# The second output projection's third and fourth chunk as a pair of seven products, with the weights in the five shared load slots

## What is computed

```python
    o = o.reshape(B, S, SB_WIDTH) * jax.nn.silu(zg)
    return o @ w_out            # 256 x 2048 by 2048 x 2048, fp32
...
        h = h + y
    return rms_norm(h, final_g)
...
        xn = rmsnorm(x, norm_mix_pre[l])
        proj = jnp.einsum('bsd,dc->bsc', xn, w_in[l])
```

## Time and profile before

| | us |
|---|---|
| three runs | 2550.94 median (2549.61 to 2550.96) |
| the profiled execution | 2550.57 |
| its span, first to last instruction | 2548.6 |
| PE busy in it | 2542.5 |
| DVE busy in it | 1865.1 |
| ACT busy in it | 1323.7 |

### The profile page before, as it was taken

How to read it: one execution, slowest core, us unless ns; L and a number is a source line. 1 busy time by engine, 2 the same in 40 slices (tenths; PEclk the granted TensorE clock), 3 DMA queues, 4 the chain that set the end, 5 groups by cost and what they waited for, 6 DMA issues and landing times.

```text
span 2548.6 us, 29599 instructions
## 1 busy us (share of the span) xinstructions
PE 2542.5 (100%) x11383; PEld 2107.5 (83%) x11383; DVE 1865.1 (73%) x2181; ACT 1323.7 (52%) x1585; POOL 34.9 (1%) x56
## 2 busy tenths in 40 slices
PE   9999999999999999999999999999999999999999
PEld 7888888888888888888888888888888888888887
DVE  6866567566866666776866876778678789899796
ACT  6654444444555555455444544445565456465563
POOL 1000000000000000000000000000020000000000
PEclk9999999999999999999999999999999999999999
DMA  8766776676787777778566787666757676667674
GB/s 282 210 204 197 210 208 193 196 207 198 209 225 201 216 195 205 219 217 231 165 183 181 206 225 198 205 206 198 241 171 230 191 212 209 218 201 230 195 229 157
DMA packets 534796, 527.43 MB, mean 207 GB/s; under 512 B 294896, under 2 KB 297824, under 8 KB 534656
## 3 DMA queue, kind: packets, MB, share of 16 engines
q1 hardware_dynamic: 531856, 518.09, 68.4%
q0 software_dynamic: 2384, 6.93, 1.1%
q10 hardware_dynamic: 416, 0.52, 0.1%
HBM read 488.24 MB, written 2.10 MB: 192 GB/s over the span
## 4 chain that ended last, share of the span: by engine, by line
PE 97%; DVE 2%; SPq 0%; DMA 0%; ACT 0%; issue 0%; DVEq 0%
PE bank L2429 29%; PE bank L2431 29%; PE bank L2430 29%; PE bank L2496 2%; PE bank L2498 2%; PE bank L2497 2%; DVE t_wl L1310 1%; PE bank L2615 1%; PE bank L2604 1%; PE bank L2594 1%; SPq L548 0%; DMA t_stage<-in_a_w_in_dram 0%; PE bank L2537 0%; PE bank L2550 0%; PE bank L2543 0%; DVE t_ytl L1359 0%
## 5 line engine op out<-in xcount | busy, mean ns | idle before, releaser
L1310 DVE TENSOR_TENSOR t_wl<-t_stage,t_wh 128x1024 fp32r<-128x1024 f32 x837 | 1012.1, 1221 | 479.8 <-ACT t_wh L726 472.8
L726 ACT ACTIVATE t_wh<-t_stage 128x1024 fp32r<-128x1024 f32 x838 | 878.0, 1057 | 753.5 <-PE bank L2431 696.9
L2429 PE MATMUL bank<-t_wl,t_xth 128*128 128x512 f32 x2320 | 909.9, 392 | 0.4 <-DVE t_xtl L1352 0.4
L2431 PE MATMUL bank<-t_wh,t_xtl 128*128 128x512 f32 x2320 | 903.0, 389 | 0.0
L2430 PE MATMUL bank<-t_wh,t_xth 128*128 128x512 f32 x2320 | 902.8, 389 | 0.0
L2431 PEld LDWEIGHTS bank<-t_wh,t_xtl 128*128 128x128 f32 x2320 | 435.5, 188 | 90.9
L2429 PEld LDWEIGHTS bank<-t_wl,t_xth 128*128 128x128 f32 x2320 | 435.6, 188 | 90.4 <-DVE t_xtl L1352 0.9
L2430 PEld LDWEIGHTS bank<-t_wh,t_xth 128*128 128x128 f32 x2320 | 435.7, 188 | 89.6 <-issue 0.2
L2429 PE MATMUL bank<-t_wl,t_yth 128*128 128x512 f32 x882 | 343.4, 389 | 0.1
L2430 PE MATMUL bank<-t_wh,t_yth 128*128 128x512 f32 x882 | 342.7, 389 | 0.0
L2431 PE MATMUL bank<-t_wh,t_ytl 128*128 128x512 f32 x882 | 342.7, 389 | 0.0
(11 more groups left out here) (441 smaller groups left out, 1810.3 us busy)
## 6 DMA issues: line engine op xcount, KB each, us to landing
t_stage<-in_a_w_in_dram SPq DMA_DIRECT2D x182, 512.0 KB, 4.4
t_stage<-in_w_in_dram SPq DMA_DIRECT2D x168, 512.0 KB, 4.2
t_stage<-in_b_w_in_dram SPq DMA_DIRECT2D x128, 512.0 KB, 4.4
t_stage<-in_w_down_dram SPq DMA_DIRECT2D x92, 512.0 KB, 5.3
t_stage<-in_w_up_dram SPq DMA_DIRECT2D x91, 512.0 KB, 4.5
t_stage<-in_a_w_out_dram SPq DMA_DIRECT2D x60, 512.0 KB, 4.4
t_ubuf<-in_w_up_dram SPq DMA_DIRECT2D x37, 512.0 KB, 4.6
t_ubuf<-in_w_down_dram SPq DMA_DIRECT2D x36, 512.0 KB, 5.3
```

What stands on the lines that cost most here:

```text
L726: e.activation(wh[:, j % N_SPLIT], stage[s], ACT.Copy).then_inc(*hi(j))
L1310: e.tensor_tensor(low, src, high.bitcast(F32), ALU.subtract).then_inc(*lo(j))
L2429: e.matmul(o, h, w_l, start=start, stop=False)
L2431: return e.matmul(o, l, w_h, start=False, stop=stop)
```

## The change

The pair is added to `halved_pairs`, `sums_of` and `quarters` name the places of its sums and its partial results (parts of `vreg` and the buffers 0 and 1), and no slots are opened for it. The work of ACT and DVE around `b_out` is put in another order, with the pieces of the `a_out` pair; the row products of chunks 2 and 3, their squares and the scales go behind the gained parts.

```diff
@@ halved_pairs
             [(("a_out", h, 2), ("a_out", h, 3)) for h in range(2)] +
+            [(("b_out", 2), ("b_out", 3))] +
@@ sums_of
+        if name[0] == "b_out":
+            return ("zg",), mtl[:, 0:4, :], mtl[:, 4:8, :], vreg[:, 5120:6144]
@@ quarters
-        if kind in ("gm", "up", "a_out"):
+        if kind in ("gm", "up", "a_out", "b_out"):
@@ scalar
-        for c in range(4):
+        def hb_squares(c):
             slot(end("b_out", c) + 2)
             e.wait_ge(*vec.at("hb", c))
             for i in range(2):
                 squares(hres[:, i, cols(c)], ssq[:, i, c:c + 1], "hb", c, i)
+
+        def final_squares(c):
             for i in range(2):
                 e.wait_ge(*vec.at("final", c, i))
                 squares(hres[:, i, cols(c)], ssq2[:, i, c:c + 1], "final", c, i)
-            slot(end("b_out", c) + (5 if c == 3 else 4))
+
+        slot(end("b_out", 0) - 2)
+        sum_high("zg")
+        hb_squares(0)
+        final_squares(0)
+        slot(end("b_out", 0) + 4)
+        gained_highs(0, gmix, "x2", 0)
+        hb_squares(1)
+        apart(first_of["b_out", 2], turned.at("zg", 3))
+        slot(end("b_out", 1) + 4)
+        gained_highs(1, gmix, "x2", 1)
+        slot(end("b_out", 1) + 7)
+        final_squares(1)
+        hb_squares(2)
+        hb_squares(3)
+        for c in (2, 3):
+            slot(end("b_out", 3) + (2, 5)[c - 2])
             gained_highs(c, gmix, "x2", c)
+        final_squares(2)
+        final_squares(3)
@@ vector
+        def to_result(m):
+
+            e.wait_ge(*vec.at("w", "pair", m))
+            for n in range(2):
+                d = hres[:, :, cols(pairs[m][n][1])]
+                e.tensor_tensor(d, d, buf[n], ALU.add).then_inc(*vec("early", m, n))
+                e.wait_ge(*vec.at("early", m, n))
+
+        slot(end("b_out", 0) - 3)
+        split_sums(yth, ytl, vreg[:, 4096:5120], vreg[:, 5120:6144], "zg")
+        slot(end("b_out", 0) - 1)
+        sum_low("zg")
+        out_sum(0)
+        out_turn(0)
+        final_row(0)
+        out_sum(1)
+        out_turn(1)
+        gained_lows(0, gmix, "x2", 0)
+        m = first_of["b_out", 2]
+        slot(end("b_out", 1) + 3)
+        together(m, turned.at("zg", 3))
+        final_row(1)
+        slot(end("b_out", 1) + 6)
+        gained_lows(1, gmix, "x2", 1)
+        slot(end("b_out", 1) + 7)
+        to_result(m)
+        out_sum(2)
+        out_turn(2)
+        out_sum(3)
+        e.wait_ge(*vec.at("hb", 3))
+        e.memset(pad[:, :, 0:3], 0.0).then_inc(*vec("pad0"))
+        out_turn(3)
+        slot(end("b_out", 3) + 2)
+        gained_lows(2, gmix, "x2", 2)
+        slot(end("b_out", 3) + 5)
+        gained_lows(3, gmix, "x2", 3)
+        final_row(2)
+        final_row(3)
...
```

More of the change, by code:

```diff
@@ L182, in _program @@
     mtl, _ = sb("mtl", [128, 16, S], F32R, offset=v_at + 16384)
-    vtile = (vreg[:, 1024:2048].rearrange("p (a b) -> p a b", a=2), vreg[:, 5120:6144].rearrange("p (a b) -> p a b", a=2))
+    vtile = [vreg[:, n:n + 1024].rearrange("p (a b) -> p a b", a=2) for n in (1024, 5120)]
     stage = [stage_[:, i] for i in range(N_STAGE)] + [ubuf[:, 0], ubuf[:, 1], spare[:, 0], spare[:, 1], pool4[:, 3], rowb,
@@ L1739, in vector, with out_sum @@
         zg_low(3)
-        for c in range(4):
+        def out_sum(c):
             slot(end("b_out", c))
@@ L1746, in vector, with out_turn @@
                 e.tensor_tensor(hr, hr, accs("b_out", c)[i], ALU.add).then_inc(*vec("hb", c) if i else vec())
-            if c == 3:
-                e.wait_ge(*vec.at("hb", 3))
-                e.memset(pad[:, :, 0:3], 0.0).then_inc(*vec("pad0"))
+        def out_turn(c):
             slot(end("b_out", c) + 1)
@@ L1752, in vector, with final_row @@
             turn_chunk(lambda i: hres[:, i, cols(c)], flat[zt_buf[c]], "x2", c)
+        def final_row(c):
             slot(end("b_out", c) + 2)
@@ L1759, in vector @@
                 e.tensor_tensor(hr, hr, rowb[:, c % 2, :], ALU.mult).then_inc(*vec("final", c, i))
[L1760 to L1776, removed]
@@ L1777, in vector @@
-            slot(end("b_out", c) + (5 if c == 3 else 4))
-            gained_lows(c, gmix, "x2", c)
+        def to_result(m):
[6 more added lines that the diff above has]
+        split_sums(yth, ytl, vreg[:, 4096:5120], vreg[:, 5120:6144], "zg")
@@ new lines, in vector @@
+        out_sum(3)
[8 more added lines that the diff above has]
+        final_row(3)
+        both = rq[:, 1, 0:4]
+        v12, v1 = both[:, 0:2], both[:, 2:4]
+        eps1 = rq[:, 0, 4:6]
+        e.tensor_reduce(v1, ssq[:, :, 0:4], AX, ALU.add).then_inc(*vec())
@@ new lines, in vector @@
+        after_own()
+        e.tensor_scalar(v1, v1, 1.0 / D, EPS, ALU.mult, ALU.add).then_inc(*vec())
+        after_own()
+        e.tensor_scalar(eps1, v1, EPS, None, ALU.mult).then_inc(*vec())
+        e.wait_ge(*square.at("final", 3, 1))
+        e.tensor_reduce(v12, ssq2[:, :, 0:4], AX, ALU.add).then_inc(*vec())
+        after_own()
+        e.scalar_tensor_tensor(out=v12, in0=v12, scalar=1.0 / D, in1=eps1, op0=ALU.mult,
+                               op1=ALU.add).then_inc(*vec())
+        rsqrt(s12_1, both, 4)
@@ L1781, in vector @@
+        after_own()
+        e.tensor_scalar(h12, s12, 0.5, None, ALU.mult).then_inc(*vec("h12"))
         slot(when(428))
```

## The result

The kernel with the pair takes **2556.32 us** (median of 14 runs, 2554.50 to 2557.66), the kernel before 2550.48 (14 runs, 2549.59 to 2551.73). The ratio is 1.0022, 95% interval 1.0015 to 1.0029: about 5.8 us slower, where +3.04 on the profiled execution was forecast. The profiled execution took 2556.42 us, with a span of 2554.7.

The account below looks back on a forecast made before the run. TensorE, busy the whole span, was taken as the bound: matmuls by their pace. -1.36 + 1.64 + 1.74 + 1.02 = +3.04 us gave 2553.6 for the profiled execution, 2554.0 as median; range 2550.3 to 2557.5.

Parts of the forecast that it names:

- The gain: PE, first four K tiles of chunks 2 and 3: 42 matmuls instead of 48, -1.36 us.
- The first wait: PE at chunk 1's last group waits for its weights' low part, whose load waits for a slot: +1.64 us.
- low part P6 after a 0.4 wait: DVE's queue after the second weight difference: product P6's low part was to come after waiting only 0.4.
- The walk: Four queues followed in program order with trace durations, from DVE's low part at 1099.39; it gave the three waits.
- The second wait: PE's `begin` at chunk 3's first group waits for chunk 1's addition, queued on DVE behind low parts: +1.74 us.
- The third wait: PE at chunk 2's group at K tile 8 waits for a low part behind DVE's queued work: +1.02 us.
- The load time: The critical loads of the first two waits: 3.8 us taken from a quiet stretch, 3.6 and 5.0 as ends.
- The moved steps: Gained parts, row products and scales of chunks 2 and 3: nothing, at most 1 to 2 us if order slips.
- All hidden: Rival: added work stays hidden as in the first output projection's pair; -1.36 to -0.4, 2549.6 to 2550.5; chance 0.12.
- The five slots cost more: Rival: loads of the first two waits land late; at 6.0 us each, +7.4, 2558.4; chance 0.22.
- The clock falls: Rival: TensorE drops to 1.2 GHz after waits; one group per wait is 8.2 more, 2562; chance 0.04.
- The tail slips: Rival: scales come late for the eviction, PE waits at the next chunk; +1.5, 2555.5 in all; chance 0.06.

Follow-up runs that it names:

- the order alone: New order of ACT's and DVE's steps without the pair, compared with the kernel before: 2550.77 us, ratio 1.0001.
- the kernel with slots and later gained parts: Changed kernel plus two extra load slots in vreg and ACT's gained high parts of chunk 0 two groups later: 2549.56 us, ratio 0.9997.
- the gained parts later: Changed kernel with one number changed, ACT's gained high parts of chunk 0 two groups later: 2553.49 us, ratio 1.0010.
- the row load late: Changed kernel with POOL's loads of the third and fourth final_g row waiting for chunk 3's addition: 2555.28 us, ratio 1.0016.
- the sum early: Kernel with the row load late, plus DVE adding chunk 1's result one group earlier: 2555.82 us, ratio 1.0017.
- the later row product: Kernel with the sum early, plus DVE's row product of chunk 1 behind its gained low parts: 2555.28 us, in the repeat 2554.58.

## Why the prediction was right or wrong

- **The gain, -1.36.** Right: six matmuls fewer on the page, a stage 1.36 shorter where nothing waits, and 1.26 less in the median.
- **The first wait, +1.64.** The mechanism is right: it is at the last group of chunk 1, released by the low part whose load waits for a slot, and two slots remove it. Its size by itself is near too (1.79 of idle time, 1.96 as a shift). But the point in time was off by 3.1 us (its low part ended at 1135.8, not 1132.7), and the step that failed is the one just ahead: "low part P6 after a 0.4 wait". That wait measured 3.47. The walk took all four transfers of the turned chunk as landing in about 3.1 us; the last took 6.5. The hint stood in the trace: ACT had already stood 2.06 at these gained parts before the change, and I walked past it as hidden, because then it was. The price is two waits nobody had forecast, 1.59 and 0.91 in shifts of starts. With them the sum would be +5.5.
- **The second wait, +1.74.** With five slots it is seen at its place wherever the clock stays up and chunk 1's sum is not moved (1.17 and 1.32), for the reason given, DVE's queue. In the profiled execution the fall of the clock took its place, at 1.74 us by chance the same figure.
- **The third wait, +1.02.** Measured 0.64 to 0.70, 0.80 as a shift. One half of the reason holds: with the addition a group earlier it takes over what the second loses. The other half stands behind it: once DVE is sooner, ACT's wait for chunk 1's transfer is next late, and the walk didn't have that.
- **The load time, 3.8.** The two critical loads landed in 3.8 and 3.7. The estimate of 3.2 from the Trainium skill, "DMA: Bandwidth & Descriptors", section "Anatomy of one DMA — SWDGE (gpsimd) path", whose fit is for GpSimd's path while SP issues these loads, would have been too short: the shortest weight load of this stage in the profiles took 3.5.
- **The moved steps, nothing.** Right: the order alone gives 2550.77, and PE waits nowhere behind chunk 3. The scales were done at 1200.0 instead of the 1196.1 forecast, 3.1 of it the stage's own extra delay (6.2 at the next chunk's start, where 3.04 was forecast).
- **The rivals.** *All hidden* is what the kernel with slots and later gained parts does, not this one. *The five slots cost more* had a late transfer in it, but at the loads; it was the turned chunk's. *The clock falls* did happen, against its 0.04, though not as worked out. It was one stretch of 3.4 us at the lower level, with 1.74 us of lost pace, and it cost about nothing net, since it covered a wait. In the 14 runs the mean granted clock was 0.999 in four and 1.0 in ten, with mean times of 2556.3 and 2556.1. *The tail slips* didn't.

The trace of the kernel before held a stronger hint at the late transfer than ACT's 2.06. There the fourth transfer of chunk 0 took 4.7 us, and that of chunk 1, with a row load issued just behind it (1135.58), took 6.6. Landing of chunk 1's four, issued from 1133.00 on:

```profile
DMA to landing us min/median/max: 2.9/3.1/6.6
```

Forecast and result differ by 2.8 us, or by 2.97 in the profiled stage. P6 and K tile 12 are 2.50 of that, the slower matmuls behind the waits 0.37, and the three other terms together 0.10 (4.50 for 4.40). That 2556.32 lies in the range that was given is in part luck: its upper part was meant for weight loads that land late, and what filled it was a transfer that the forecast had no term for. The rise lies about at the 5.1 us that the forecast called the least that can be told from no change (the interval is 3.8 to 7.4 us); to more than that it gave 0.27.

Two things stay open. One is why the fourth transfer is late. With GpSimd's row load just behind it, it took 6.5, 6.4 and 6.8, but 5.4 with the order alone and 4.8 with the gained parts later; with the row load moved away, 4.2 to 4.8 in each of eight profiles. So the row load is part of it, not all. The weight load issued 0.9 us behind it is a candidate that no run took away, but it isn't enough by itself: at chunks 1 to 3 of the same profiles, with a weight load 0.7 to 1.3 us behind it and no row load within 0.4 us, the fourth transfer landed in 3.0 to 3.7. With a row load issued within 0.4 us of it, it took 4.7 to 6.8, at chunks 0 to 2, in the kernel before too. Why chunk 0's takes 4.2 to 4.8 without one is not shown. The Trainium skill, "DMA: Bandwidth & Descriptors", section "Issuing engines are not separate DMA queues", says that transfers share the same engines and interleave whichever engine starts them, and the row load's effect agrees with that. The other is what a median holds beyond the stage of its profile: 0.6 with the row load late, 1.0 with the sum early, and 0.7 less than the stage in the repeat of the later row product. PE has waits elsewhere that come and go from one execution to the next (the profile of the order alone, with none in the stage, is 1.8 above its median), and one profile of each kernel can't say more.

## What to carry to other kernels

Where an engine that runs its queue in order is given an instruction that waits for a transfer, everything behind it waits for that transfer's landing too. Walk the queue once with the longest landing that the trace shows, not with the median: here 6.6 us stood in the trace of before, and 3.1 was taken. Put such an instruction behind the work that the bottleneck asks for next; here one number bought 3 of 6 us. The pair saves matmuls at the price of load slots, and came out ahead here only with two more of them. A wait taken away from a backlog came back at the next consumer, as the early sum showed.

## What the runs showed of the hardware

TensorE's granted clock fell to 1.2 GHz for 3.4 us although PE stood still for no longer than 2.1 us at a time: behind waits of 1.43, 0.60 and 1.79 with groups of matmuls between them (changed kernel), and behind 0.61 and 2.09 in one profile of the kernel with the later row product. In its second profile, with 0.61 and 1.79, it stayed up, as it did for 0.31 and 1.87. The Trainium skill, "TensorE: Matmul & The Clock Gate", section "Why this matters for your kernels", warns of idle gaps between bursts; here several short ones close together went with the fall. While the clock is low, PE's busy time grows, so a page that shows more busy time for fewer matmuls is a reason to ask for the clock by windows: the tenths of the page still read 9. It is no proof of a fall: the second profile of the later row product has 2544.2 us of busy PE without one, for 2544.4 in the changed kernel, and there it is matmuls behind several short waits.
